# Half of a sequence's cached latents gathered a second time, already turned, for the scores of the sample attention

## The chip, the cores and the metric

The kernel runs on one core of one Trainium2 chip. A core has five engines that run side by side and hand work to one another through semaphores: TensorE (PE) multiplies matrices, VectorE (DVE) and ScalarE (ACT) work on rows of elements, GpSimd (POOL) here does little but issue gathers, and SyncE (SP) issues plain transfers. On-chip data lies in SBUF (128 partitions), matmul results in PSUM. The metric is the device time of one execution in microseconds (us).

## The reference

One inference step of a two-layer decoder, all in float32, for a prompt of 512 tokens and for 8 sample sequences of one token each. Layer 0 is a convolution branch and a gated linear attention, layer 1 a multi-head latent attention, and each is followed by PEER, a retrieval of single-neuron experts. The change is in layer 1, in the attention of the samples over 4096 cached positions. These lie in 32 pages of 128 rows; a page table says which physical page holds which logical one. Cut to what matters:

```python
ckv_past = cache_ckv[j][page_table].reshape(bs, -1, R_KV)     # (8, 4096, 256)
kpe_past = cache_kpe[j][page_table].reshape(bs, -1, D_ROPE)   # (8, 4096, 32)
sp = (einsum('bqhr,bkr->bhqk', q_lat, ckv_past)               # scores: needs r on the partitions
      + einsum('bqhd,bkd->bhqk', q_pe, kpe_past)) * MLA_SCALE
p = softmax(concatenate([sp, s_self]))
o = einsum('bhqk,bkr->bqhr', p[..., :n_past], ckv_past) + ... # weighted sum: needs k on the partitions
```

A matmul sums over the partitions. The scores sum over r, so they want the latents turned (r on the partitions), while the weighted sum wants the rows as they lie in the cache (k on the partitions).

## The kernel before

The stages run one after the other, each a function with its own buffers and semaphores, and a barrier of all engines between them: the layer-0 mixer, PEER, `latent_projections` (buffers `c_`), `latent_sample` (buffers `d_`), PEER again.

**Gathers.** `gather_past(b)` brings a whole sequence b (4.7 MB) into one of three buffers of `smp_past`, with four indirect DMAs issued by POOL, each for eight pages: 128 rows of 9216 bytes (eight keys with their latents and rope keys). The row numbers are worked out near the start of `latent_projections`: the page table comes by DMA, DVE casts it (L1935), PE spreads it over the partitions (L2102), DVE makes row numbers of it (L1937); DVE's `turn_in(0)` (L1864) and PE's first projection come behind that in their queues. At the end of that stage, when the prompt's attention no longer needs `smp_past`, POOL gathers sequences 0 to 2.

**The sample stage.** `latent_sample` walks over b = 0..7. PE's program of one step, in order (each engine's queue is strictly in order):

- `turn_rope(b)` (L2461) turns the rope keys; it waits for all four gathers of sequence b
- `turn_pages(b, g)` for g = 0..7 (L2469): eight 128x128 transposes each, into one of two PSUM turn banks; ACT (L2294, g = 0, 2, 4, 7) or DVE (L2359, g = 1, 3, 5, 6) copies the result into `ckvT`
- between them, what is left of the softmax of sequence b-1: `fold_heads(b-2)`, `turn_max(b-1)` (L2492), `spread_max(b-1)` (L2498)
- `scores(b, 0)` behind g = 5 (L2481 on the latents, L2485 on the rope keys); it waits until ACT has taken the exponentials of b-1 (L2304), which free the score bank
- `turn_weights(b-1)` (L2506), g = 6 and 7, `total_sums(b-1)`, `weighted(b-1)` (L2528, L2529), and last `scores(b, 1)`

DVE takes the largest score (`partial_max`, L2364) after `scores(b, 1)`; before it stands `normed(b-1)`, which scales the result of `weighted(b-1)`. POOL waits until `weighted(b-3)` is done (semaphore `o_ps`) and then issues the four gathers of sequence b into the buffer that this frees. SP loads the output weights into such a buffer when `weighted(5)` is done. After the loop comes the rest of sequence 7 and the output projection (L2588, L2594).

Of the kernel before, what the change touches and what calls it, by code (L numbers as in the profile page):

```python
# [15 lines left out]
I32 = mybir.dt.int32  # L16
# [1611 lines left out]
def latent_projections(nc, w, out, ident, x_sb, smp):  # L1628

    with ExitStack() as ctx:  # L1630
        def sb(name, shape, dt=F32):
# [25 lines left out]
        table_f = sb("table_f", [PAST_PIECE, NB])  # L1657
        spread = sb("spread", [PAST_PIECE, 128])
# [7 lines left out]
        mask = sb("mask", [128, SEQ])  # L1666
        eps = sb("eps", [128, 1])
# [30 lines left out]
            "s_ps", "max_ready", "e_ready", "sum_inv", "p_ready", "pT_ps", "pT_ready", "pv_ps", "o_used", "y_ps", "y_used"))  # L1698
        stores = [sem("stores_even"), sem("stores_odd")]
# [15 lines left out]
        def _(sp):  # L1715
# [3 lines left out]
            for dst, name in ((table, "page_cols"), (spread, "spread"), (part, "sixteenth")):  # L1719
                sp.dma_start(dst[:], w[name]).then_inc(table_in, 16)  # L1720
# [128 lines left out]
        def _(dve):  # L1849
# [84 lines left out]
            dve.wait_ge(table_in, 48)  # L1934
            nc.vector.tensor_copy(table_f[:], table[:]).then_inc(table_ready, 1)  # L1935
# [48 lines left out]
        def _(pe):  # L1984
# [117 lines left out]
            nc.tensor.matmul(ps[0][:, 0:NB], spread[:], table_f[:], start=True, stop=True).then_inc(ids_ps, 1)  # L2102
# [53 lines left out]
def latent_sample(nc, w, ident, x_sb, smp):  # L2156
# [6 lines left out]
    TURNS = G + 2  # L2163
    CKV_BUFS = 6
    with ExitStack() as ctx:
# [26 lines left out]
        ckvT = sb("ckvT", [128, CKV_BUFS, 2, KEYS])  # L2192
# [15 lines left out]
        y_row = sb("y_row", [B, D_MODEL])  # L2208
# [10 lines left out]
        def buf(g):  # L2219
            return ckvT[:, g % CKV_BUFS]  # L2220

# [8 lines left out]
        oT_ps, oT_ready, y_ps, y_rows, y_used = sem("oT_ps"), sem("oT_ready"), sem("y_ps"), sem("y_rows"), sem("y_used")  # L2230
        block = ctx.enter_context(nc.Block())
        KPE, PT = 0, 7
        GROUP_TURN = (1, 2, 3, 4, 5, 6, 8, 9)
# [31 lines left out]
        @block.gpsimd  # L2265
        def _(pool):
            nc.gpsimd.memset(one[:], 1.0).then_inc(consts, 1)
            nc.gpsimd.memset(self_s[:], NEG_MASK).then_inc(consts, 1)
            nc.gpsimd.memset(self_e[:], 0.0).then_inc(consts, 1)
            for b in range(BUFS, B):  # L2270
                pool.wait_ge(o_ps, b - BUFS + 1)
                gather_past(nc, w, smp, b)

        @block.scalar
        def _(act):
# [39 lines left out]
            for b in range(B):  # L2315
                page_out(b, 0)
                if b == 0:
                    latent_queries_out()
                page_out(b, 2)
                if b:  # L2320
                    exps(b - 1)
                page_out(b, 4)
                if b:
                    weights_out(b - 1)
                page_out(b, 7)
# [9 lines left out]
        def _(dve):  # L2335
# [59 lines left out]
            for b in range(B):  # L2395
                rope_out(b)
                if b >= 2:
                    folded(b - 2)
                page_out(b, 1)
                if b:  # L2400
                    largest(b - 1)
                page_out(b, 3)
                page_out(b, 5)
                page_out(b, 6)
                if b == 0:
                    self_out()
                if b:
                    normed(b - 1)
                partial_max(b)
# [10 lines left out]
        def _(pe):  # L2420
# [25 lines left out]
            def turn_free(i, b, half):  # L2446

                before = i - 4 if b == 0 and i == PT + 2 else i - 2
# [23 lines left out]
            def scores(b, half):  # L2472

                for g in range(4 * half, 4 * half + 4):
                    pe.wait_ge(*turned(GROUP_TURN[g], b))
# [3 lines left out]
                for c in range(2):  # L2479
                    for j in range(4):  # L2480
                        nc.tensor.matmul(s_bank[group(j), KEYS * half:KEYS * half + KEYS], qlT[:, c, b, :], buf(4 * half + j)[:, c, :], start=(c == 0), stop=False)  # L2481
# [61 lines left out]
            for b in range(B):  # L2543
# [21 lines left out]
                turn_pages(b, 4)  # L2565
                turn_pages(b, 5)
# [3 lines left out]
                turn_pages(b, 6)  # L2570
                turn_pages(b, 7)
# [3 lines left out]
                scores(b, 1)  # L2575
# [22 lines left out]
PAST_BUFS, PAST_PIECE, PAST_PIECES = 3, 8, NP // 8  # L2598
ROW = PAST_PIECE * (R_KV + D_ROPE)


def sample_buffers(nc, ctx):

    def sb(name, shape, dt=F32):
# [4 lines left out]
            "row_ids": sb("row_ids", [128, DEC_BATCH * PAST_PIECES], I32), "four": sb("four", [128, 4]),  # L2609
# [4 lines left out]
def constants():  # L2614
# [3 lines left out]
    for l in range(LEVELS):  # L2618
# [25 lines left out]
            "low_half": np.stack([p % 32 < 16, p % 32 >= 16], axis=1).astype(np.float32),  # L2644
            "sixteenth": (p % TOPK).astype(np.float32)[:, None]}


def laid_out(a):
# [12 lines left out]
    def low_rows(g):  # L2661
# [19 lines left out]
        "cache_rows": lambda: np.concatenate([a["cache_ckv"][0].reshape(-1, 8 * R_KV), a["cache_kpe"][0].reshape(-1, 8 * D_ROPE)], axis=1),  # L2681
        "page_cols": lambda: np.ascontiguousarray(a["page_table"].reshape(-1, 8).T),
# [17 lines left out]
_USED = ['ab_norm_cols', 'ab_w_in', 'ab_w_out', 'c_kv_norm', 'c_norm_cols', 'c_w_in', 'c_w_out', 'c_w_uk', 'c_w_uv', 'cache_rows', 'causal', 'chan_cols', 'conv_w_cols', 'cos2', 'ffn_norm', 'final_norm', 'fold', 'fold_h', 'four', 'gate_b_cols', 'gla_head_g', 'gate_rows', 'ident', 'iota16', 'keysT', 'level_masks', 'low_half', 'own_col32', 'own_row', 'own_row32', 'page_cols', 'peer_uv0', 'peer_uv1', 'q_norm_cols', 'sin2', 'sixteenth', 'spread', 'spread8', 'state_conv', 'state_conv_cols', 'state_gla', 'turn_q', 'w_q_heads', 'w_qx', 'w_ukT', 'x_prompt', 'x_sample']  # L2700
# [21 lines left out]
```

## Time and profile before

| | |
|---|---|
| median of 3 runs | 3503.63 us (3503.6 to 3508.55) |
| profiled execution, its span from first to last instruction | 3501.1 us |
| the sample stage within it | about 1928.3 to 2150.0 us |
| POOL's gathers in the whole program | 1040 of PEER, 32 of the past |

The span is given from the first to the last instruction; the runs' time is taken by the device around it, so the fastest and the median run lie 2.5 us above it. In the views below a time of start counts from the start of the span. "[x <-Y]" behind an instruction says that its engine was idle for x us before it and that Y ended the wait; "issue" means that nothing the profile shows was waited for, "remote" that the semaphore's last update could be put down to no instruction.

### The profile page before, as it was taken

The numbers are of one execution on the slowest core, as the hardware profiler recorded it, in microseconds if no ns is written. First come the engines' busy times: TensorE is split into PE (matmuls) and PEld (weight loads), VectorE is DVE, ScalarE is ACT, GpSimd is POOL, SyncE is SP. The second block draws the span as 40 slices with busy tenths as digits, with TensorE's granted clock in tenths as the row PEclk, the third lists the DMA queues.
The fourth block names the chain that finished last, engine by engine and source line by source line (L and its number), as shares of the span: only waits on it lengthen the run. The fifth ranks groups of instructions, "written<-read, shape, count | busy, mean of one in ns | idle before, by whom it ended". The sixth has DMA issues, their size and how long they took to land. (4 is left out here: it accounts for less than half of the span.)

```text
span 3501.1 us, 34014 instructions
## 1 busy us (share of the span) xinstructions
PE 2983.7 (85%) x10561; PEld 1480.5 (42%) x10561; DVE 2185.4 (62%) x5266; ACT 1438.0 (41%) x4182; POOL 1301.9 (37%) x1112
## 2 busy tenths in 40 slices
PE   8987888888889888887999886888888888888886
PEld 7653333433334433333554764434333434433332
DVE  4874667666667766664362334666766676766765
ACT  3122445444444544443351222444444444544444
POOL 0211444444544444452001010445444454444442
PEclk9988999999999999999999897999999999999999
DMA  4015999999999999998203345999999999999998
GB/s 163 29 52 228 421 421 414 421 421 415 420 398 421 418 421 421 421 419 350 81 1 162 134 165 220 421 421 414 421 421 421 415 408 421 409 421 421 421 419 355
DMA packets 178372, 1194.53 MB, mean 341 GB/s; under 512 B 22320, under 2 KB 28240, under 8 KB 38150
## 3 DMA queue, kind: packets, MB, share of 16 engines
q0 software_dynamic: 154368, 1128.34, 77.8%
q1 hardware_dynamic: 22525, 63.11, 4.8%
q8 instruction: 84, 1.38, 0.2%
q10 hardware_dynamic: 1296, 0.90, 0.1%
q14 instruction: 99, 0.80, 0.1%
HBM read 1188.29 MB, written 4.46 MB: 341 GB/s over the span
## 5 line engine op out<-in xcount | busy, mean ns | idle before, releaser
L1581 PE MATMUL p_acc<-p_rows,p_diag 128*128 128x512 f32 (+1 forms) x4160 | 1973.0, 616 | 412.8 <-ACT p_diag L1184 411.0
L1414 DVE CUSTOM_DVE_ANT_0 p_rows<-p_rows,p_x_n 128x1024 f32<-128x1024 f32 x1024 | 1243.7, 1223 | 790.5 <-DMA p_rows<-in_peer_uv,p_ids 788.4
L1096 POOL DMA_INDIRECT p_rows<-in_peer_uv,p_ids x1024 | 1217.0, 1188 | 1384.6 <-PE p_acc L1581 1281.6
L1581 PEld LDWEIGHTS p_acc<-p_rows,p_diag 128*128 128x128 f32 (+1 forms) x4160 | 752.9, 192 | 1508.5 <-ACT p_diag L1184 790.8
L1178 ACT ACTIVATE p_acts<-p_dots 128x1 f32<-128x1 f32 x1040 | 208.3, 200 | 871.8 <-DVE p_dots L1414 870.4
L1184 ACT ACTIVATE p_diag<-ident,p_gated 128x128 f32<-128x128 f32 x1024 | 410.9, 401 | 33.6
L1180 ACT ACTIVATE p_gated<-p_acts,p_gates 128x1 f32<-128x1 f32 x1024 | 301.6, 295 | 33.2
L1531 PE MATMUL p_q_bank<-p_w_q,p_xT 128*128 128x256 f32 x1024 | 234.9, 383 | 2.2 <-ACT p_xT L1127 2.2
L1531 PEld LDWEIGHTS p_q_bank<-p_w_q,p_xT 128*128 128x128 f32 x1024 | 196.1, 192 | 55.5 <-issue 28.5
L1150 ACT COPY p_q_rows<-p_q_bank 128x256 f32<-128x256 f32 x68 | 25.2, 370 | 347.7 <-PE p_q_bank L1531 347.7
L1623 POOL DMA_INDIRECT smp_past<-in_cache_rows,smp_row_ids x32 | 30.0, 937 | 361.1 <-PE c_ps L2096 227.4
L1178 ACT ACT_TABLE_LOAD x73 | 93.7, 1283 | 8.7 <-DVE p_dots L1414 7.5
L2469 PE MATMUL d_turn<-ident,smp_past 128*128 128x128 f32 x512 | 78.0, 311 | 15.6 <-DVE d_kpeT L2353 14.4
L541 DVE SCALAR_TENSOR_TENSOR a_conv<-a_u,a_conv_wc,a_conv 128x512 f32<-128x512 f32 x120 | 86.6, 792 | 0.0
L688 PE MATMUL a_ps<-a_xT,a_w_in 128*128 128x260 f32 x384 | 85.7, 384 | 0.1
L1414 DVE DVE_READ_ACCUMULATOR2_ANT p_dots<- 128x1 f32 x1040 | 85.1, 82 | 0.0
L1170 ACT ACT_TABLE_LOAD x64 | 82.1, 1283 | 1.1
L688 PEld LDWEIGHTS a_ps<-a_xT,a_w_in 128*128 128x128 f32 x384 | 72.5, 190 | 11.9 <-issue 0.4
L2469 PEld LDWEIGHTS d_turn<-ident,smp_past 128*128 128x128 f32 x512 | 68.8, 162 | 19.9 <-DVE d_kpeT L2353 16.3
L2359 DVE COPY d_ckvT<-d_turn 128x512 f32<-128x512 f32 x64 | 42.1, 687 | 56.2 <-PE d_turn L2469 56.1
L2294 ACT COPY d_ckvT<-d_turn 128x512 f32<-128x512 f32 x64 | 34.7, 587 | 103.0 <-PE d_turn L2469 103.0
L1088 POOL MEMSET p_eps<- 128x1 f32 x2 | 0.2, 98 | 171.2 <-POOLq L62 171.2
(402 smaller groups left out, 2483.0 us busy)
## 6 DMA issues: line engine op xcount, KB each, us to landing
p_w_q<-in_w_q_heads SPq DMA_DIRECT2D x16, 1024.0 KB, 12.2
p_rows<-in_peer_uv,p_ids POOLq DMA_INDIRECT x1024
a_w_in<-in_ab_w_in SPq DMA_DIRECT2D x6, 1024.0 KB
a_w_in<-in_ab_w_out SPq DMA_DIRECT2D x1, 4096.0 KB
c_arena<-in_c_w_out SPq DMA_DIRECT2D x1, 4096.0 KB, 12.7
smp_past<-in_c_w_out SPq DMA_DIRECT2D x1, 4096.0 KB
a_w_in<-in_ab_w_in SPq DMA_DIRECT2D x4, 1008.0 KB, 21.3
smp_past<-in_w_qx SPq DMA_DIRECT2D x1, 3072.0 KB, 18.6
```

What stands on the lines that cost most here:

```text
L541: ins = nc.vector.scalar_tensor_tensor(out=conv[:, c, 0:SEQ], in0=u[:, c, i:i + SEQ], scalar=conv_wc[:, c, i:i + 1], in1=conv[:, c, 0:SEQ] ...
L688: last = nc.tensor.matmul(ps[bank][:, 512 * b:512 * b + half], w_in[:, k, at:at + 128], xT[:, k, half_of(b)], start=(k == 0), stop=(k == K ...
L1096: nc.gpsimd.indirect_dma_start(out=rows[:, slot % RING, :], out_offset=None, in_=w[f"peer_uv{layer}"], in_offset=bass.IndirectOffsetOnAxis ...
L1170: nc.scalar.activation(ex[:], rel[:], ACT.Exp, accum_out=ex_sum[:]).then_inc(ex_ready, 1)
L1178: nc.scalar.activation(acts[:, i % 4, j:j + 1], dots[:, i % 4, j:j + 1], ACT.Gelu).then_inc(gelud, 1)
L1180: nc.scalar.mul(gated[:, i % 4, j:j + 1], acts[:, i % 4, j:j + 1], gate[:, j:j + 1]).then_inc(gated_ready, 1)
L1184: nc.scalar.mul(diag[:, i % 4, j, 0:n], unit[:], gated[:, i % 4, j:j + 1]).then_inc(diag_ready, 1)
L1414: nc.vector.tensor_tensor_reduce(rows[:, k % RING, 0:D_MODEL], rows[:, k % RING, 0:D_MODEL], x, 1.0, 0.0, ALU.mult, ALU.add, dots[:, slot ...
L1531: last = nc.tensor.matmul(q_bank[:, 0:D_KEY], xT[:, k, :], w_q[:, h, k, :], start=(k == 0), stop=(k == KC - 1))
L1581: last = nc.tensor.matmul(acc[done % 2][0:n, at], diag[:, slot // GROUP % 4, j, 0:n], rows[:, (slot + j) % RING, D_MODEL + 512 * b:D_MODEL ...
L2359: nc.vector.tensor_copy(buf(g)[:, half, :], bank(0, half)).then_inc(turn_dve, 1)
L2469: last = nc.tensor.transpose(turn[i % 2][:, KEYS * c + 128 * a:KEYS * c + 128 * a + 128], latent(b, NQ * g + a, c), ident[:])
```

## The change

The host lays out one more table, `cache_turned`: every page turned, so that row `128 * page + r` holds latent component r of the page's 128 keys (1 KB: both halves of the 256 components, keys ordered by their place in a group of eight). Of every sequence, logical pages 16 to 31 are gathered a second time from this table, 128 rows of 1 KB for each page, into three buffers `turned_c` of eight pages. `scores(b, 1)` reads them in place through an access pattern of runs of 16 elements; `scores(b, 0)` is as before.

- Gone: `turn_pages(b, 4)` to `(b, 7)`, 32 transposes and their four copies on ACT and four on DVE, in each of the eight steps. The numbers of the turns change with them.
- Added: 16 indirect DMAs of 128 KB a sequence on POOL, 128 in all. The first 24 (pieces 0 to 2) stand at the start of the sample stage. Pieces 2b+3 and 2b+4 wait for both scores of step b. **The four gathers of sequence b+2 now stand behind these 16 in POOL's queue.**
- Moved: `scores(b, 1)` stands before `weighted(b-1)`, and `partial_max(b)` before `normed(b-1)`.
- In `latent_projections`: two more small loads on SP (`lane` and a broadcast of the page numbers) ahead of `norm_col`, a wait for all five, and on DVE a cast and a multiply-add for the 128x128 row numbers. Three small tiles move into memory that is free at that time.

```diff
-            for dst, name in ((table, "page_cols"), (spread, "spread"), (part, "sixteenth")):
-                sp.dma_start(dst[:], w[name]).then_inc(table_in, 16)
+            for dst, name in ((table, "page_cols"), (spread, "spread"), (part, "sixteenth"), (lane, "lane")):
+                sp.dma_start(dst[:, :], w[name]).then_inc(table_in, 16)
+            sp.dma_start(smp["turned_ids"][:], w["turned_pages"].to_broadcast([128, 128])).then_inc(table_in, 16)
...
-            dve.wait_ge(table_in, 48)
-            nc.vector.tensor_copy(table_f[:], table[:]).then_inc(table_ready, 1)
+            dve.wait_ge(table_in, 80)
+            nc.vector.tensor_copy(table_f, table[:]).then_inc(table_ready, 1)
+            nc.vector.tensor_copy(pages_f, smp["turned_ids"][:]).then_inc(pages_ready, 1)
+            dve.wait_ge(pages_ready, 1)
+            nc.vector.tensor_scalar(smp["turned_ids"][:], pages_f, 128.0, lane[:], ALU.mult, ALU.add)
...
+        def turned_slots(b, j, c):
+            piece = 2 * b + j // 2
+            by_slot = turned_c[:, piece % TURNED_BUFS].rearrange("p g (c s q) -> p c s g q", c=2, s=KEYS_8)
+            return by_slot[:, c, NQ * (j % 2):NQ * (j % 2) + NQ]
...
-            for b in range(BUFS, B):
-                pool.wait_ge(o_ps, b - BUFS + 1)
-                gather_past(nc, w, smp, b)
+            def gather_turned(piece):
+                if piece >= TURNED_BUFS:
+                    pool.wait_ge(s_ps, 2 * ((piece - TURNED_BUFS) // 2 + 1))
+                for k in range(KEYS_8):
+                    at = KEYS_8 * piece + k
+                    nc.gpsimd.indirect_dma_start(out=turned_c[:, piece % TURNED_BUFS, k, :], out_offset=None, in_=w["cache_turned"],
+                                                 in_offset=bass.IndirectOffsetOnAxis(ap=smp["turned_ids"][:, at:at + 1], axis=0)
+                                                 ).then_inc(turned_in[piece % TURNED_BUFS], 16)
+            for piece in range(TURNED_BUFS):
+                gather_turned(piece)
+            for b in range(B):
+                for piece in (2 * b + TURNED_BUFS, 2 * b + TURNED_BUFS + 1):
+                    if piece < 2 * B:
+                        gather_turned(piece)
+                if BUFS <= b + 2 < B:
+                    pool.wait_ge(o_ps, b)
+                    gather_past(nc, w, smp, b + 2)
...
             def scores(b, half):
-                for g in range(4 * half, 4 * half + 4):
-                    pe.wait_ge(*turned(GROUP_TURN[g], b))
+                if half == 0:
+                    for g in range(4):
+                        pe.wait_ge(*turned(GROUP_TURN[g], b))
+                else:
+                    for piece in (2 * b, 2 * b + 1):
+                        pe.wait_ge(turned_in[piece % TURNED_BUFS], 16 * KEYS_8 * (piece // TURNED_BUFS + 1))
...
-                turn_pages(b, 4)
-                turn_pages(b, 5)
                 scores(b, 0)
                 if b:
                     turn_weights(b - 1)
-                turn_pages(b, 6)
-                turn_pages(b, 7)
+                scores(b, 1)
                 if b:
                     total_sums(b - 1)
                     weighted(b - 1)
-                scores(b, 1)
```

## Rows read from the trace of the kernel before

**Rows 1.** Page: the span and the engines' busy time.

```profile
span 3501.1 us, 34014 instructions
PE 2983.7 (85%) x10561; PEld 1480.5 (42%) x10561; DVE 2185.4 (62%) x5266; ACT 1438.0 (41%) x4182; POOL 1301.9 (37%) x1112
```

**Rows 2.** Windows: us; busy PE, PEld, DVE, ACT, POOL; PE's clock, DMA share, GB/s.

```profile
1973.00:1998.00 25.00, 21.90 (x261) 16.48 (x257) 9.29 (x19) 6.99 (x16) 3.75 (x4) 0.93 0.49 190
...
2098.60:2118.00 19.40, 19.40 (x255) 14.69 (x248) 9.07 (x18) 6.99 (x16) 0.00 (x0) 1.00 0.56 217
```

**Rows 3.** Timeline of POOL: start us, us, engine, instruction, idle time before it.

```profile
1884.65 0.94 POOL L1623 DMA_INDIRECT smp_past<-in_cache_rows,smp_row_ids  x1 [0.30 <-issue]
1928.35 0.09 POOL L2267 MEMSET d_one<- 1x1 f32 x1 [42.76 <-POOLq L62]
...
1998.04 0.94 POOL L1623 DMA_INDIRECT smp_past<-in_cache_rows,smp_row_ids  x1 [19.71 <-PE d_o L2529]
...
2001.77 0.94 POOL L1623 DMA_INDIRECT smp_past<-in_cache_rows,smp_row_ids  x1 [0.31 <-issue]
```

**Rows 4.** Timeline of DVE and PE beside these gathers.

```profile
1884.90 1.22 DVE L1981 TENSOR_TENSOR x_sb<-x_sb,c_ps 128x1024 f32<-128x1024 f32 x1 [14.02 <-PE c_ps L2152]
...
1997.87 0.48 DVE L2389 TENSOR_SCALAR d_o_n<-d_o,d_inv 128x256 f32<-128x256 f32 x1 [3.71 <-PE d_o L2529]
...
1998.92 1.44 PE L2485 MATMUL d_s<-d_kpeT,d_qpT 128*32 128x128 f32 x32
...
2003.85 1.23 DVE L2364 TENSOR_REDUCE d_m<-d_s 128x1 f32<-128x1024 f32 x1 [5.50 <-remote]
```

**Rows 5.** Waits in the sample stage: us in total, times, longest.

```profile
DVE d_m L2364 <- remote: 27.5, 5, 5.5
```

**Rows 6.** The 20 gathers of 1973 to 2078 us, from issue to landing.

```profile
DMA to landing us min/median/max: 8.1/9.7/11.4
```

**Rows 7.** Timeline of step 7, the last, with no gather beside it.

```profile
2101.10 1.09 PE L2461 MATMUL d_turn<-ident,smp_past 128*128 128x128 f32 x8
...
2106.37 0.38 PE L2498 MATMUL d_m<-d_one,d_nmx 1*128 1x1 f32 x2
...
2106.68 1.97 PE L2469 MATMUL d_turn<-ident,smp_past 128*128 128x128 f32 x16
...
2106.97 1.12 ACT L2304 ACTIVATE d_sc<-d_s,d_nbias 128x1024 f32<-128x1024 f32 x1
...
2108.57 1.92 PE L2481 MATMUL d_s<-d_ckvT,d_qlT 128*32 128x512 f32 x16
...
2111.30 1.09 PE L2506 MATMUL d_turn<-ident,d_sc 128*128 128x128 f32 x8
...
2114.09 0.28 PE L2517 MATMUL d_m<-d_sums,d_fold 128*128 128x2 f32 x2
...
2118.47 0.48 DVE L2389 TENSOR_SCALAR d_o_n<-d_o,d_inv 128x256 f32<-128x256 f32 x1 [3.70 <-PE d_o L2529]
...
2119.52 1.44 PE L2485 MATMUL d_s<-d_kpeT,d_qpT 128*32 128x128 f32 x32
...
2120.89 0.62 PE L2540 MATMUL d_m<-d_fold_h,d_o_n 128*128 128x16 f32 x4
...
2122.74 0.27 PE L2492 MATMUL d_m<-ident,d_m 128*1 128x128 f32 x1 [1.23 <-DVE d_olT L2393]
```

**Rows 8.** Timeline of the start of `latent_projections`.

```profile
1644.30 0.35 SPq L1720 DMA_DIRECT2D c_part<-in_sixteenth  x1
...
1649.72 0.17 DVE L1935 CAST c_table_f<-c_table 8x32 f32<-8x32 int32 x1 [2.75 <-DMA c_part<-in_sixteenth]
...
1650.61 0.25 DVE L1937 TENSOR_SCALAR smp_row_ids<-c_ps,c_part 128x32 int32<-128x32 f32 x1 [0.72 <-PE c_ps L2102]
```

**Rows 9.** Transfers: KB each, us to landing.

```profile
c_kv_gain<-in_c_kv_norm SPq DMA_DIRECT2D x1, 128.0 KB, 8.0
```

**Rows 10.** Page, the costliest groups: busy us, mean ns, idle before.

```profile
L1096 POOL DMA_INDIRECT p_rows<-in_peer_uv,p_ids x1024 | 1217.0, 1188 | 1384.6 <-PE p_acc L1581 1281.6
```

More of the change, by code:

```diff
@@ L1656, in latent_projections @@
         table = sb("table", [PAST_PIECE, NB], I32)
-        table_f = sb("table_f", [PAST_PIECE, NB])
-        spread = sb("spread", [PAST_PIECE, 128])
+        table_f = past[0:PAST_PIECE, kT_at + 128:kT_at + 128 + NB]
+        spread = past[0:PAST_PIECE, kT_at + 256:kT_at + 384]
         part = sb("part", [128, 1])
@@ L1666, in latent_projections @@
         mask = sb("mask", [128, SEQ])
+        lane = sb("lane", [128, 1])
+        pages_f = past[:, kT_at:kT_at + 128]
         eps = sb("eps", [128, 1])
@@ L2101, in _ @@
             pe.wait_ge(table_ready, 1)
-            nc.tensor.matmul(ps[0][:, 0:NB], spread[:], table_f[:], start=True, stop=True).then_inc(ids_ps, 1)
+            nc.tensor.matmul(ps[0][:, 0:NB], spread, table_f, start=True, stop=True).then_inc(ids_ps, 1)
             pe.wait_ge(ids_ready, 1)
@@ L2162, in latent_sample @@
     KEYS = NQ * 128
-    TURNS = G + 2
-    CKV_BUFS = 6
+    TURNS = G // 2 + 2
+    HALF = G // 2
     with ExitStack() as ctx:
@@ L2191, in latent_sample @@
         self_s = sb("self_s", [128, B, B])
-        ckvT = sb("ckvT", [128, CKV_BUFS, 2, KEYS])
+        ckvT = sb("ckvT", [128, HALF, 2, KEYS])
+        turned_c = sb("turned_c", [128, TURNED_BUFS, KEYS_8, R_KV])
         kpeT = sb("kpeT", [128, G, 128])
@@ L2230, in latent_sample @@
         oT_ps, oT_ready, y_ps, y_rows, y_used = sem("oT_ps"), sem("oT_ready"), sem("y_ps"), sem("y_rows"), sem("y_used")
+        turned_in = [sem(f"turned_in{i}") for i in range(TURNED_BUFS)]
         block = ctx.enter_context(nc.Block())
-        KPE, PT = 0, 7
-        GROUP_TURN = (1, 2, 3, 4, 5, 6, 8, 9)
+        KPE, PT = 0, 5
+        GROUP_TURN = (1, 2, 3, 4)
         def turn_count(i, b, half):
@@ L2446, in turn_free @@
             def turn_free(i, b, half):
-                before = i - 4 if b == 0 and i == PT + 2 else i - 2
+                before = i - 2
                 if before >= 0:
@@ L2480, in scores @@
                     for j in range(4):
-                        nc.tensor.matmul(s_bank[group(j), KEYS * half:KEYS * half + KEYS], qlT[:, c, b, :], buf(4 * half + j)[:, c, :], start=(c == 0), stop=False)
+                        dst = s_bank[group(j), KEYS * half:KEYS * half + KEYS]
+                        if half == 0:
+                            nc.tensor.matmul(dst, qlT[:, c, b, :], buf(j)[:, c, :], start=(c == 0), stop=False)
+                        else:
+                            nc.tensor.matmul(dst.rearrange("h (s g q) -> h s g q", s=NQ, g=KEYS_8), qlT[:, c, b, :], turned_slots(b, j, c), start=(c == 0), stop=False)
                 for a in range(NQ):
@@ L2598 @@
 PAST_BUFS, PAST_PIECE, PAST_PIECES = 3, 8, NP // 8
+TURNED_BUFS = 3
 ROW = PAST_PIECE * (R_KV + D_ROPE)
```

18 lines of the change are left out of this document (9 added, 9 removed).

## The prediction

> **What bounds the kernel now.** I read the page first [rows 1]: PE is busy for 85% of the span, but that is an average over stages that have different limits, and the change touches one stage of some 220 us. So the windows of that stage came next [rows 2]. A step with gathers beside it takes 25.0 us, PE busy for 21.9; the last step, with none, takes 19.4 us and PE is never idle. PE is the bound, and something that comes with the gathers costs 5 to 6 us a step. POOL works 3.75 us of a step. It is nowhere near a limit.
>
> The timelines say what the 5 us are [rows 3, 4]. PE ends the last matmul of scores(2, 1) at 2000.4 us, DVE's maximum, which waits for nothing else, starts at 2003.85, after 5.5 us of idle time. POOL ended its fourth gather at 2002.71, 1.1 us earlier. All five such steps look alike (27.5 us of DVE idle time in all [rows 5]); what holds PE's word back I cannot tell from the trace. It is no fixed price of a POOL that is issuing: during the first twelve gathers DVE started its addition at 1884.90, right after PE, while POOL was inside a gather [rows 3, 4].
>
> The third thing to read is POOL's pitch [rows 3]: gathers back to back start (2001.77 - 1998.04) / 3 = 1.243 us apart, 0.94 of it work.
>
> **What the change removes.** 32 of 64 page transposes a step. At full clock 16 of them take 1.97 us [rows 7], so PE saves 3.9 us. Of that only part shortens the step. Pages 4 and 5 hid the exponentials of the step before: spread_max ends at 2106.75, ACT's exponentials run 2106.97 to 2108.1, and scores(b, 0) began at 2108.57 in any case. Without the pages it waits for ACT and begins at 2108.2. From there 2.7 us of scores, 1.3 of turned weights and 3.0 of scores(b, 1): from the start of turn_rope(b) to the end of scores(b, 1) I get 14.1 us. With 4.1 for total_sums and weighted(b-1), until its last matmul has ended (2114.09 to 2118.4) a step of PE is 18.2 us, against some 19.8 before (2101.10 to 2120.96). The 16 copies a step on ACT and DVE lie beside it and give nothing.
>
> **What it adds.** 16 gathers a step. A 1 KB row is in no row of POOL's; PEER's gathers of 8 KB rows and these of 9 KB take the same 0.94 us when nothing stretches them (PEER's mean of 1.19 is of all of its gathers, whatever runs beside them) [rows 3, 10], so I take 0.94 and a pitch of 1.243. Lower bound: the 0.3 us between two gathers alone. Upper bound: PEER's mean, pitch 1.49. **20 gathers are 24.9 us a step on POOL: POOL, not PE, sets the step.** The transfers themselves are small (128 KB every 1.24 us).
>
> **Where it hurts: the queue.** Before, the four gathers of sequence b+2 were issued as soon as weighted(b-1) was done, a whole step ahead. Now they stand behind 16 others, and turn_rope(b+2) waits for all four. POOL starts in the sample stage at 1928.7 (three memsets after 1928.35). Ahead of the gathers of sequence 7 stand 24 + 6 x 16 + 4 x 4 = 136 gathers: 169.0 us, so 2097.7. The fourth is issued 3.7 us later and lands 11.4 us after that (the longest, since POOL's queue is full around it) [rows 6]: 2112.8. Another 14.1 us of PE: scores(7, 1) end at 2126.9. Before they ended at 2119.52 + 1.44 = 2120.96 [rows 7]. **+5.9 us.**
>
> This supposes that POOL never waits. From the first gather of sequence b+2 to the end of scores(b+2, 1) is 3.7 + 11.4 + 14.1 = 29.2 us; POOL's own work in the same time is 24 gathers, 29.8. There are 0.6 us to spare. But PE now stands idle for some 6 us of each step, and behind idle time the granted clock falls to 1.2 GHz: in a step in which PE was idle for 3.1 us it was 0.93 over 25.0 us [rows 2], half speed for 3.5 us, which loses some 1.7 us of work; twice as long would lose 3.4. I take 2.5. Then the path misses POOL by 1.9 us; such a delay is carried through every second step (3 and 5), and the low clock counts once more in step 7: 2 x 1.9 + 2.5 = **+6.3 us** (0 to 9.0).
>
> **The moved lines.** weighted(6) now stands between scores(7, 1) and the last softmax. Before, turn_max(7) came 1.8 us after the scores [rows 7]; now 4.1 of sums and weighted, 0.5 of DVE's scaling, 0.6 of fold_heads and a copy (0.3, an estimate) [rows 7] come first, with the hand-overs 5.9. **+4.1 us.** What follows is unchanged. The output weights (4 MB) are loaded when weighted(5) is done, now about 2110, while the gathers of sequence 7 are still landing; 3.5 us shared would cost up to 3.5, I take **+2**.
>
> **The first stage.** DVE started on the page table when the third small load had landed, 5.4 us after its issue, which took 0.35 [rows 8]. Two more loads issued before the wait: some +0.8. The new DVE work (a 128x128 cast and a multiply-add) hides in the 0.72 us in which DVE waits for PE's spread of the table. The broadcast of the page numbers may be slower: kv_gain, the nearest one, took 8.0 us to land [rows 9], which would make it +3.4. I take **+1**. PE's first projection waits behind this.
>
> **How the strided read counts.** scores(b, 1) reads runs of 16 elements. If that halved PE's rate on its latents, 1.9 us more [rows 7], it would count like the clock, 3 times: +5.7. No row shows it; I take 0 and keep 5.7 for the range.
>
> **Sum.** 5.9 + 6.3 + 4.1 + 2 + 1 = 19.3 us on a span of 3501.1, and with 2.5 us between span and median 3503.6 + 19.3 = **3523 us**. The case's own range is 5.9 + 4.1 + 0.8 = 10.8 to 5.9 + 9.0 + 4.1 + 3.5 + 3.4 + 5.7 = 31.6: 3514 to 3535.
>
> **The rivals.** *POOL's issue is cheap (faster).* If a gather of short rows costs POOL little more than the 0.3 us gap, PE sets the step: scores(0, 1) at about 1954, seven steps of 18.2 end at 2081, 39.5 us before today; with 4.1 and 1 given back 3469. It decides where the pitch falls below about 1.05: 139 gathers times 0.19 are the 26 us between my sum and -7. Against it: every unstretched gather in the trace is 0.94, for two row sizes. 0.08. The Trainium skill leans this way: DMA: Bandwidth & Descriptors, in its anatomy of one DMA, calls descriptor generation "small, variable" and says that many descriptors can be emitted before the cost shows. The trace doesn't agree for POOL's time, 0.94 us for 128 rows.
>
> *Only POOL's count binds (no change to tell).* If the four gathers land 6 us sooner than 11.4, the last piece sets the end: 148 x 1.243 = 184.0, landed by about 2115.4, scores 3.0: 2118.4, which is -2.6; with 4.1 and 1: 3506. Against it: 8.1 is the shortest landing of any, and the fourth is always the latest. 0.13.
>
> *PE's word is held back during the new gathers too (much slower).* If PE's signals to ACT and DVE were stuck until 1.1 us after POOL's last gather in all of this stage, a step would be 20.7 us of 16 gathers, 6 of the four, then 13 of PE: 40 us instead of 25. Five such steps, with 34 and 24 for the two shorter ones and the first from about 1983, end at 2241: 3628. For it: five of five in this stage. Against it: the addition at 1884.90. 0.11.
>
> *DVE stretches the gathers (slower).* At PEER's mean pitch of 1.49, 139 x 0.25 = 35 us more: 3558. Against it: DVE's scaling from PSUM (L2389) ran beside the first of the four gathers, which kept 0.94 [rows 3, 4]; the other four steps repeat this. 0.06. The Trainium skill's SBUF — State Buffer, under who interferes with whom, says that DVE's copies can take the port that GpSimd writes its descriptors through; no copy of the stage lies beside a gather in this trace.
>
> **How the numbers follow.** My forecast has 0.62. Within 0.2% (7 us, about what a measurement of this kernel can tell) I put 0.11: the second rival, less its upper edge. Faster 0.09, the first rival and a little of the second. Slower 0.80. The range leaves out most of the first, all of the third and half of the fourth rival: 3497 to 3548.
>
> **What would show it.** POOL: gathers 1.24 us apart with hardly a gap from 1928.7 to about 2115, of 0.94 us each. PE: its longest wait in steps 3 to 7 is before turn_rope(b), for the landing of the gathers of the past, and not before scores(b, 1) for the turned pieces. The clock is at half speed behind it. DVE's maximum starts right behind the scores again. Scores(b, 1) take the same 3 us as scores(b, 0). In `latent_projections` the cast starts about 1 us later. I am wrong if the pitch is under 1.05 (faster), if PE waits for the turned pieces alone (about no change), or if the idle time "remote" grows with POOL's bursts (much slower).

## The result, and the profile after

The changed kernel takes 3613.67 us (median of 4 runs), the kernel before beside it 3505.35 us. The ratio is 1.0309, 95% interval 1.0294 to 1.0324: 3.1% slower. I had forecast slower, by 19 us; it is 108. The time lies near my third rival (3628 us, chance 0.11).

The page's span, and of the waits those of 1928 to 2261 us (us in total, times, longest):

```profile
span 3612.7 us, 33562 instructions
...
ACT d_ckvT L2326 <- remote: 128.0, 5, 26.5
DVE d_o_n L2419 <- remote: 117.4, 6, 21.5
```

These answer to [rows 1, 5]. By the page PE is busy for 2995.5 us, 12 us more than before; POOL, at 1423.1, has 121 us more of work, which is not on the path. Before, words of PE that came late cost DVE 27.5 us. Now they cost ACT 128 us and DVE 117, side by side. The windows of a step with all 20 gathers (us; busy PE, PEld, DVE, ACT, POOL; PE's clock, DMA share, GB/s) answer to [rows 2]:

```profile
2049.70:2087.55 37.85, 20.89 (x222) 13.85 (x222) 6.52 (x14) 5.05 (x12) 18.89 (x20) 0.77 0.52 181
```

37.9 us instead of 25.0 for less work of PE, DVE and ACT. The timeline of one step, with the engines sorted together (start us, us, instruction, idle time before it):

```profile
2011.51 1.22 DVE L2394 TENSOR_REDUCE d_m<-d_s 128x1 f32<-128x1024 f32 x1 [21.39 <-PE d_s L2521]
2011.75 0.94 POOL L2292 DMA_INDIRECT d_turned_c<-in_cache_turned,smp_turned_ids  x1 [9.76 <-PE d_s L2521]
2017.44 0.38 PE L2565 MATMUL d_o<-smp_ckv,d_self_pT 128*32 128x256 f32 x1 [0.79 <-issue]
2024.61 0.37 PE L2497 MATMUL d_turn<-ident,smp_past 128*128 128x128 f32 x1 [1.03 <-issue]
...
2030.50 0.95 POOL L2292 DMA_INDIRECT d_turned_c<-in_cache_turned,smp_turned_ids  x1 [0.30 <-issue]
...
2034.65 0.48 DVE L2419 TENSOR_SCALAR d_o_n<-d_o,d_inv 128x256 f32<-128x256 f32 x1 [21.45 <-remote]
2034.75 1.07 ACT L2326 COPY d_ckvT<-d_turn 128x512 f32<-128x512 f32 x2 [26.50 <-remote]
2034.81 0.94 POOL L1623 DMA_INDIRECT smp_past<-in_cache_rows,smp_row_ids  x1 [3.36 <-remote]
...
2049.70 1.22 DVE L2394 TENSOR_REDUCE d_m<-d_s 128x1 f32<-128x1024 f32 x1 [7.72 <-PE d_s L2521]
```

Read it in this order. DVE's maximum and POOL's first gather start right behind the scores. PE ends weighted(b-1) at 2017.8, the rope keys and the first group of pages by 2025.0, and then waits for DVE's scaling of weighted(b-1). ACT has nothing to do and starts on that first group at 2034.75; DVE's scaling of a result that PE ended at 2017.8 starts at 2034.65; POOL's wait for the same word ends at 2034.81. Three engines go on within 0.2 us of one another, 3.2 us after POOL's last gather of the run, on words that PE owed them: from the end of weighted(b-1) to DVE's scaling it is 16.8 us here and 17.5 us in the step that begins at 2125.25. From the first gather to that moment it is 22.9 us for 16 gathers. It was 5.8 us for the four of [rows 3, 4]. It is 34.2 for the run of 24 with which the stage begins, and 11.7 for the last run of eight:

```profile
1931.88 0.96 POOL L2292 DMA_INDIRECT d_turned_c<-in_cache_turned,smp_turned_ids  x1 [0.43 <-issue]
1966.09 1.29 DVE L2389 COPY d_ckvT<-d_turn 128x512 f32<-128x512 f32 x2 [30.07 <-remote]
...
2202.49 0.95 POOL L2292 DMA_INDIRECT d_turned_c<-in_cache_turned,smp_turned_ids  x1 [11.64 <-PE d_s L2521]
2214.23 0.48 DVE L2419 TENSOR_SCALAR d_o_n<-d_o,d_inv 128x256 f32<-128x256 f32 x1 [10.28 <-remote]
```

That is 1.43 to 1.47 us for each gather of a run, where POOL needs 1.25. PE's own matmuls suffer too: from 2016 us on they start in clumps with gaps of 0.2 to 1.0 us in which PE waits for nothing that the profile shows.

### The profile page after: what moved, and what is told of

It is laid out like the page before. It is cut to its first block and busy times, and to the rows that moved or that the text cites. A ratio compares the mean times of both kernels' runs of the same rounds, so it can differ in the third digit from the quotient of the medians.

```text
span 3612.7 us, 33562 instructions
## 1 busy us (share of the span) xinstructions
PE 2995.5 (83%) x10305; PEld 1470.2 (41%) x10305; DVE 2166.4 (60%) x5236; ACT 1421.6 (39%) x4150; POOL 1423.1 (39%) x1240
## 5 line engine op out<-in xcount | busy, mean ns | idle before, releaser
L2292 POOL DMA_INDIRECT d_turned_c<-in_cache_turned,smp_turned_ids x128 | 121.1, 946 | 119.6 <-PE d_s L2521 82.6
L2326 ACT COPY d_ckvT<-d_turn 128x512 f32<-128x512 f32 x32 | 18.0, 588 | 183.2 <-remote 128.0
L2497 PE MATMUL d_turn<-ident,smp_past 128*128 128x128 f32 x256 | 55.7, 370 | 23.9 <-issue 23.3
L1154 ACT COPY p_qT<-p_q_bank 128x256 f32<-128x256 f32 x64 | 23.8, 372 | 90.0 <-PE p_q_bank L1545 89.8
## 6 DMA issues: line engine op xcount, KB each, us to landing
p_w_q<-in_w_q_heads SPq DMA_DIRECT2D x16, 1024.0 KB, 12.1
```

What stands on the lines that cost most here:

```text
L2292: nc.gpsimd.indirect_dma_start(out=turned_c[:, piece % TURNED_BUFS, k, :], out_offset=None, in_=w["cache_turned"], in_offset=bass.Indirect ...
L2497: last = nc.tensor.transpose(turn[i % 2][:, KEYS * c + 128 * a:KEYS * c + 128 * a + 128], latent(b, NQ * g + a, c), ident[:])
```

## The experiments

They ran in five jobs, each on one chip with the kernel before beside it. The kernel before told two kinds of job apart: 3505.9, 3505.5 and 3502.1 us in three, 3477.2 and 3477.1 us in two. One chip ran a job of either kind, so the kind isn't a property of the chip, as the expectations had it. I call the three *stuck* and the two *free*, for what the traces show. In the last of the three only kernels with spaced gathers have a trace; that it is a stuck one rests on the kernel before, 3502.1 us beside them, and on words of PE up to 1.0 us late in the changed kernel with fills, where the same kernel in the free jobs has 0.1. A ratio is to the kernel before of the same job.

**What the change does where nothing is stuck.** Both kernels, unchanged, ran again, in a stuck and in a free job.

> The kernel before, unchanged, to have its profile beside runs of the changed one on one chip. The runs so far were on two chips: on one the kernel before took 3505.9 us, on the other 3477.2, and on that other one a kernel with four gathers in a row at 1.25 us showed no late words of PE. Chip theory: whether PE's words get stuck during POOL's gathers is a property of the chip. On a chip of the first kind this profile shows five waits of DVE of 5.5 us for a late word and some 3504 us, on one of the second kind none, steps of 19.8 us and some 3477 us.

> The changed kernel, unchanged. On a chip of the first kind 3613 us, steps of 38 us and PE's words 10 to 17 us late. On one of the second kind nothing holds PE's words; what is left is POOL's pace, 20 gathers x 1.25 = 25 us a step, and the gathers of the past behind the turned ones: by the prediction's own sum scores(7, 1) end at about 2127 to 2133 and the kernel takes 3510 to 3520, slower than the kernel before there by 35 to 40 us, since that one loses nothing to late words.

Measured, in a stuck job: 3505.2 and 3612.0 us (ratio 1.0308, 1.029 to 1.0325), as in the first result. The kernel before has five waits of DVE of 5.5 us, and the changed one words of PE up to 17.9 us late.

> The changed kernel, unchanged, once more, for the chip of the second kind, on which it has not run (its mark is a time of some 3477 us of the kernel before beside it). There, if late words of PE are all that my forecast missed, the profile shows no word of PE more than 1 us late, POOL's gathers 1.25 us apart with hardly a gap, PE's longest waits before turn_rope for the gathers of the past, and scores(7, 1) ending at about 2127 to 2133; the kernel takes 3505 to 3520. On a chip of the first kind 3612 us again.

> The kernel before, for its profile on the same chip as the run above. On a chip of the second kind: no wait of 5.5 us of DVE for a late word, steps of 19.8 us throughout, 3477 us. On one of the first kind 3505 us.

Measured, in a free job: 3476.7 us for the kernel before, 3521.6 us for the changed one (1.0124, 1.0107 to 1.0141). Steps of the kernel before, at DVE's maximum, in the free job (the timeline):

```profile
1979.22 1.23 DVE L2364 TENSOR_REDUCE d_m<-d_s 128x1 f32<-128x1024 f32 x1 [2.08 <-PE d_s L2485]
1999.01 1.23 DVE L2364 TENSOR_REDUCE d_m<-d_s 128x1 f32<-128x1024 f32 x1 [2.10 <-PE d_s L2485]
```

19.8 us with gathers beside them, as the one without had in [rows 7]: the 5.5 us of [rows 4] are gone, and the kernel is 28 us faster by that alone. Of the changed kernel in the free job, PE's longest wait, POOL's only waits of the stage, the landing of all 32 gathers of the past, and the last maximum:

```profile
PE d_turn L2489 <- DMA smp_past<-in_cache_rows,smp_row_ids: 35.2, 13, 7.0
...
2030.42 0.95 POOL L2292 DMA_INDIRECT d_turned_c<-in_cache_turned,smp_turned_ids  x1 [1.71 <-PE d_s L2521]
2081.40 0.94 POOL L2292 DMA_INDIRECT d_turned_c<-in_cache_turned,smp_turned_ids  x1 [1.30 <-PE d_s L2521]
...
DMA to landing us min/median/max: 6.1/11.1/23.9
...
2135.57 1.23 DVE L2394 TENSOR_REDUCE d_m<-d_s 128x1 f32<-128x1024 f32 x1 [7.72 <-PE d_s L2521]
```

No word of PE is more than 0.2 us late. Here the steps of my working are to be seen: POOL is the bound and waits twice, 1.7 and 1.3 us, behind the scores of steps 3 and 5; PE waits for the gathers of the past; the last scores end at 2135.5, where I had 2126.9 + 6.3 = 2133.2. Of the 20 gathers of this stage the landing is 6.1/10.0/14.2 us; the 23.9 belongs to the twelve before it. The kernel ends at 3521.6; the forecast was 3523.

**Is it the pitch of the gathers?** POOL gets a fill behind each of the four gathers in the kernel before; `pacer` only waits for its own last fill before the next.

```diff
                 pool.wait_ge(o_ps, b - BUFS + 1)
-                gather_past(nc, w, smp, b)
+                gather_past(nc, w, smp, b, pace)     # behind each gather: nc.gpsimd.memset(idle[:], 0.0), 128 x 512
```

> The kernel before, with a fill of 128x512 zeros on POOL behind each of the four gathers of sequences 3 to 7, so that they start some 1.8 us apart instead of 1.24. If a gather takes some 1.4 us of the way that PE's words need, and the words are stuck only because gathers come faster than that, they now pass between the gathers: a step falls from 25.0 to some 20 us, the kernel to about 3480. If the words are stuck for as long as POOL's run lasts, whatever its pitch, the run is 2 us longer and so is the step: about 3513.

Measured, in a stuck job: 3480.7 us, ratio 0.9931 (0.9915 to 0.9948). The gathers start 1.64 us apart and DVE's maxima 20.5:

```profile
1977.08 0.94 POOL L1637 DMA_INDIRECT smp_past<-in_cache_rows,smp_row_ids  x1 [47.42 <-PE d_o L2547]
1978.72 0.94 POOL L1637 DMA_INDIRECT smp_past<-in_cache_rows,smp_row_ids  x1 [0.16 <-issue]
...
2000.75 1.23 DVE L2382 TENSOR_REDUCE d_m<-d_s 128x1 f32<-128x1024 f32 x1 [2.83 <-PE d_s L2503]
2021.27 1.22 DVE L2382 TENSOR_REDUCE d_m<-d_s 128x1 f32<-128x1024 f32 x1 [2.83 <-PE d_s L2503]
```

The word is 1.0 us late instead of 3.6. More work for POOL, in a longer run of gathers, gives 25 us: the run's length doesn't hold the words. That it is the distance between the gathers, and not something else that a fill between them does, is how I read it; no run made the distance without a fill.

> The kernel before with a fill of 128x256 instead of 128x512 behind each of the four gathers: they start some 1.38 us apart, between 1.24 (words stuck, step 25.0 us) and 1.64 (words at most 1.0 us late, step 20.5 us). If a gather takes 1.42 us of the way that the words need, gathers at 1.38 still fill it and the words stay stuck nearly as long: 3495 to 3505. If only the idle time between two gathers counts, the words are late by about half as much: near 3490. If any fill in between frees the way, 3480.

Measured: 3477.0 us, 0.9999 (0.999 to 1.0009). It fell into a free job, where nothing is stuck at 1.25 us either. It says nothing of the bound between 1.25 and 1.64.

The same in the changed kernel, three fills of 128x64 behind each gather of the stage:

> The changed kernel with three small fills of 128x64 zeros on POOL behind every gather of the sample stage, 144 gathers in all, so that they start some 1.6 to 1.8 us apart instead of 1.25. POOL gets slower by 50 to 70 us over the stage. If PE's words and matmuls are stuck only while gathers follow each other faster than about one in 1.42 us, they now get through, POOL alone sets the step (20 x 1.7 = 34 us against 38) and the kernel is faster than the changed one all the same: 3560 to 3595. If the words are stuck in any run of gathers, the runs are now 27 us long instead of 20 and the kernel slower: 3650 or more.

> The changed kernel with three small fills behind each gather, so that they start 1.69 us apart. On the chip of the second kind it took 3579 us and POOL's pace set the step, 33.8 us. If on a chip of the first kind the fills free PE's words, it takes the same 3579 us there, 33 us less than the changed kernel although POOL is slower. If a run of gathers holds the words whatever its pitch, 3650 or more there.

> The changed kernel with gathers 1.69 us apart, once more, now hoping for a chip of the first kind (3505 us of the kernel before beside it), on which it has not run. If the wider pitch frees PE's words there, some 3579 us, as on two chips of the second kind, and faster than the changed kernel's 3612 us with a slower POOL; no word of PE more than 1 us late. If the words are held in any run of gathers, whatever its pitch, 3650 us or more.

Measured: 3579.0 and 3578.3 us in the two free jobs, 3578.7 us in a stuck one (1.0216, 1.0199 to 1.0233). The stuck one:

```profile
2034.04 0.95 POOL L2310 DMA_INDIRECT d_turned_c<-in_cache_turned,smp_turned_ids  x1
2035.72 0.95 POOL L2310 DMA_INDIRECT d_turned_c<-in_cache_turned,smp_turned_ids  x1
...
PE d_turn L2508 <- DMA smp_past<-in_cache_rows,smp_row_ids: 73.9, 20, 9.8
```

The kind of job no longer matters. With a POOL that needs 1.68 us a gather the changed kernel is 33 us faster in a stuck job than with one that needs 1.25, and what PE waits for is the gathers of the past, 74 us in all. In a free job the same fills cost 57 us. Both signs come from the same edit: this is the experiment that separates stuck words from POOL's pace. The 33 us compare two stuck jobs, since the changed kernel without fills had no run beside this one.

**Is it the queue?** The gathers of the past ahead of the turned ones:

```diff
             for b in range(B):
+                if BUFS <= b + 2 < B:
+                    pool.wait_ge(o_ps, b)
+                    gather_past(nc, w, smp, b + 2)
                 for piece in (2 * b + TURNED_BUFS, 2 * b + TURNED_BUFS + 1):
                     if piece < 2 * B:
                         gather_turned(piece)
-                if BUFS <= b + 2 < B:
-                    pool.wait_ge(o_ps, b)
-                    gather_past(nc, w, smp, b + 2)
```

> The changed kernel with one line of POOL's program moved: in each step the four gathers of sequence b+2 are issued before the 16 of turned pages. Queue theory (the prediction's: the gathers of the past are late because they stand behind the turned ones): their delay and the low clock behind it go, 5.9 + 6.3 us back, 3601. Held-word theory (the words that PE sends to ACT and DVE are stuck until POOL's whole run of gathers is over): the run is now 20 gathers without a gap and begins only when weighted(b-1) has ended, some 4 us later; the words come about 1.42 x 20 = 28.4 us after its first gather instead of 22.8, so a step is some 8 to 10 us longer and the kernel slower than the changed one: 3645 to 3665.

> The changed kernel with the gathers of sequence b+2 ahead of the turned ones. On a chip of the first kind 3617 us. On one of the second kind POOL still needs 25 us a step, but the four gathers of the past land early and the step is POOL's 25 us plus its wait for weighted(b-1): by the queue theory no longer than in the changed kernel, 3500 to 3515.

Measured, both in stuck jobs: 3617.6 us (1.0319, 1.0302 to 1.0337) and 3618.4 us (1.0323). Neither theory's number. The queue theory falls in a stuck job: what it moves isn't what binds. In a free job this order had no run, so there the queue is read from the trace and wasn't varied. But a run of 20 gathers doesn't hold all words to its end either. The run that starts at 2054.60 us:

```profile
2060.28 0.58 ACT L2326 COPY d_ckvT<-d_turn 128x512 f32<-128x512 f32 x1 [3.38 <-PE d_turn L2497]
2061.72 0.58 ACT L2326 COPY d_ckvT<-d_turn 128x512 f32<-128x512 f32 x1 [0.85 <-remote]
2063.17 0.69 DVE L2389 COPY d_ckvT<-d_turn 128x512 f32<-128x512 f32 x1 [4.35 <-remote]
2066.02 0.16 ACT L2330 COPY d_nbias<-d_m 128x1 f32<-128x1 f32 x1 [3.71 <-remote]
...
2073.82 0.27 PE L2521 MATMUL d_s<-d_kpeT,d_qpT 128*32 128x128 f32 x1 [1.06 <-issue]
2075.22 0.27 PE L2521 MATMUL d_s<-d_kpeT,d_qpT 128*32 128x128 f32 x1 [1.13 <-issue]
```

PE had executed all that these copies wait for by 2059.7. Its words come out one at a time, 1.4 us apart at first and 0.7 to 2.1 us after that (DVE's second copy starts at 2065.31), and later matmuls start singly, 1.4 and 2.1 us apart. So PE isn't shut off; what it sends, and then what it executes, comes some 0.7 us or a multiple of it apart while gathers follow one another closely. My picture "held until the run is over" may be this, seen where PE had much to send; no run shows that the two are one.

**What is PE's saving worth?** Only the first three pieces gathered:

```diff
             for b in range(B):
-                for piece in (2 * b + TURNED_BUFS, 2 * b + TURNED_BUFS + 1):
-                    if piece < 2 * B:
-                        gather_turned(piece)
...
-                        pe.wait_ge(turned_in[piece % TURNED_BUFS], 16 * KEYS_8 * (piece // TURNED_BUFS + 1))
+                        pe.wait_ge(turned_in[piece % TURNED_BUFS], 16 * KEYS_8)
```

> The changed kernel without the turned gathers behind the first three pieces: scores(b, 1) of the later sequences read old pieces, so the scores of their second half are not computed from their own latents. PE, ACT and DVE execute what they do in the changed kernel. It prices PE's saving alone. Queue theory and held-word theory both expect the steps to fall from 38 us; if the four gathers of the past still hold PE's words for 3 to 4 us a step, the step is about 23.5 us and the time about 3530; if PE alone sets it, 18.2 us a step and about 3493. If the changed kernel's loss were in PE's own program (the strided read, the moved lines), the time would stay above 3580.

Measured, in a stuck job: 3499.9 us (0.9985, 0.9976 to 0.9995). The windows of step 1, of the last step and of one with the four gathers:

```profile
1979.89:1993.69 13.80, 11.90 (x150) 8.39 (x148) 5.56 (x11) 4.96 (x12) 0.00 (x0) 1.00 0.01 2
2099.83:2117.71 17.88, 16.30 (x222) 11.37 (x222) 6.58 (x14) 4.96 (x12) 0.00 (x0) 1.00 0.62 237
2035.94:2056.83 20.89, 17.75 (x222) 11.62 (x222) 6.58 (x14) 4.87 (x12) 3.75 (x4) 0.92 0.58 227
```

13.8 us without weighted(b-1), 17.9 with it: I had 14.1 and 18.2. PE's program is as short as worked out; four gathers in a row still cost 3.0 us of each step, and the first run of 24 some 25 us.

**Another engine for the gathers.** SP loads a page's row number into a register and issues a plain transfer; POOL keeps the four gathers of a step.

```diff
+                    for k in range(KEYS_8):
+                        at = KEYS_8 * piece + k
+                        row = nc.values_load(smp["turned_ids"][0:1, at:at + 1], engines=[SP], ...)
+                        sp.dma_start(turned_c[:, piece % TURNED_BUFS, k, :], w["cache_turned"][bass.ds(row, 128), :]).then_inc(turned_in[piece % TURNED_BUFS], 16)
```

> The changed kernel with the turned pages fetched by SP instead of POOL: for each page SP loads its row number into a register and issues one plain transfer of 128 rows of 1 KB. POOL is left with the four gathers of a step, as before. Held-word theory: only those four hold PE's words, the first scores no longer wait for a run of 24 gathers, and a step is 18 to 24 us: 3465 to 3506, if SP manages 16 pages in a step. If loading a number and issuing take SP more than 1.2 us a page, SP sets the step: at 1.65 us a page 26.4 us a step, about 3520. If the turned transfers themselves (not POOL's issuing) hold PE, the time stays near 3600.

Measured, in a stuck job: 3506.7 us (1.0008, 0.9998 to 1.0018), 107 us less than the changed kernel. The same bytes reach the same place, so it is the issuing on POOL and not the moving of these bytes that holds PE. POOL's four gathers of a step, 1.25 us apart, still do: words of PE up to 2.4 us late. What is left is SP's pace (timeline, transfers of a stretch in one row) and PE's wait for a turned piece:

```profile
1929.61 26.77 SPq L2279 DMA_DIRECT2D d_turned_c<-in_cache_turned  x24
...
1994.76 3.34 PE L2514 MATMUL d_s<-d_turned_c,d_qlT 128*32 128x512 f32 x16 [3.97 <-issue]
```

26.77 us for 24 pages, 1.1 us each. With the eight numbers of a piece loaded by one instruction ahead of the wait:

> The kernel in which SP fetches the turned pages, with the eight row numbers of a piece loaded by one instruction ahead of the wait, instead of one by one between the transfers. In the run with single loads SP spent 1.1 us on a page, and PE waited 3 to 4 us a step for the turned pieces. If that pitch was what PE waited for, a page now takes 0.5 us and the step falls from 24.5 to about 21 us, as in the kernel without turned transfers: some 3480. If the pieces come late because the 4.7 MB of the past go ahead of them in the DMA engines, the step stays at 24 us: about 3505.

> The same, and POOL's four gathers of a step spaced by three small fills. If both causes add, the words of PE are no longer stuck and the step is near PE's own 18 us: 3460 to 3470. If the past's transfers hold up the turned ones, 3480 to 3490, as fast as the kernel before with spaced gathers.

Measured, in a free job: 3471.6 us (0.9984, 0.9974 to 0.9994) and 3471.2 us (0.9981). A page now takes 15.0 / 24 = 0.62 us, the steps are 17.9 us, and spacing adds nothing where nothing is stuck. The last step is 25.3 us; in `sp_batch`:

```profile
1932.74 14.98 SPq L2280 DMA_DIRECT2D d_turned_c<-in_cache_turned  x24
...
2065.82 0.39 SPq L2291 DMA_DIRECT2D smp_past<-in_c_w_out  x1
...
2082.71 3.24 PE L2515 MATMUL d_s<-d_turned_c,d_qlT 128*32 128x512 f32 x16 [6.08 <-issue]
```

PE stands for 6.1 us before scores(7, 1): the last piece is behind 4 MB of output weights. The next edit puts the weights behind it.

```diff
             for b in range(B):
-                if b == B - 2:
-                    sp.wait_ge(o_ps, B - 2)
-                    sp.dma_start(w_out, ...).then_inc(wout_in, 16)
                 sp_gather(p for p in (2 * b + TURNED_BUFS, 2 * b + TURNED_BUFS + 1) if p < 2 * B)
+            sp.wait_ge(o_ps, B - 2)
+            sp.dma_start(w_out, ...).then_inc(wout_in, 16)
```

> The kernel in which SP fetches the turned pages with numbers loaded eight at a time, with the load of the output weights behind the last turned piece instead of before it. Where that kernel took 3471.6 us its last step was 25.3 us instead of 17.9, and PE waited 6.3 us in it for the last turned piece, which stands behind 4 MB of weights in SP's queue. If that is the reason, the last step falls to about 18 us: 3464 to 3466 on a chip of the second kind, and some 20 us more on one of the first kind, where the four gathers of the past hold PE's words for 2 to 3 us a step.

> The fastest version put together: SP fetches the turned pages, the output weights come behind the last of them, and three small fills space POOL's four gathers of a step. Without the fills it took 3486.0 us on a chip of the first kind, with PE's words up to 4.0 us late and five steps of 21.7 to 23.0 us instead of 17.9. If spacing frees the words, 3464 to 3468 on either kind of chip.

> The version put together, once more. On a chip of the second kind it took 3461.5 us. On one of the first kind, where it took 3486.0 us with PE's words up to 4.0 us late before the four gathers of a step were spaced, it should take 3462 to 3468 us, 1.2% less than the kernel before, if spacing frees the words.

Measured: without fills 3486.0 us in a stuck job (0.9945, 0.9929 to 0.9962), the last step 17.9 us, so the weights were the reason, and words of PE at most 2.5 us late by its trace, where the expectation of the next run says 4.0; with them 3461.5 us in a free one (0.9954, 0.9937 to 0.997) and 3461.3 us in a stuck one (0.9883, 0.9867 to 0.99). In the stuck one:

```profile
2023.31 1.23 DVE L2409 TENSOR_REDUCE d_m<-d_s 128x1 f32<-128x1024 f32 x1 [7.72 <-PE d_s L2536]
2041.19 1.23 DVE L2409 TENSOR_REDUCE d_m<-d_s 128x1 f32<-128x1024 f32 x1 [7.72 <-PE d_s L2536]
```

17.9 us a step (one of them 18.1), in either kind of job the fastest version of all: 16 us below the kernel before where no word is stuck, and 41 us where they are, if POOL neither issues the turned gathers nor its own back to back. Of the 41 us the turned pages are the smaller part: spacing POOL's gathers alone gave the kernel before 25 us in a stuck job (`paced_before`).

## Why the prediction was wrong

**The step that failed** is the supposition under "Where it hurts" that only POOL's count and the queue set the time, with PE's words free during the new gathers: late words are a term that the sum has at nothing. I gave the case in which they are late 0.11. It gave 40 us a step and 3628; measured are 38 us and 3613.7, with words of PE up to 17.5 us late in five steps. Of the 40 us, 20.7 for the run of 16 is 22.9; the 6 us for the four gathers of the past don't appear, since PE's next words pass during them (DVE and ACT start on PE's transposes at 2037.20 and 2039.12 while they are issued or just behind); and PE's 13 us are 15, part of them at half clock.

**Why I gave it so little.** For it stood five runs of gathers out of five in this very stage; against it one addition of DVE in another stage [rows 4]. Beside that one PE executes long matmuls, 128x512, and sends DVE a word in some 14 us; here it executes matmuls of 128x128, some 0.12 us each, besides the long ones, and sends several words a step. The stage in which the new gathers were to lie had only witnesses for it. I let one from elsewhere outweigh them because I had no mechanism.

**The queue (+5.9, +6.3).** Not what binds in the result. In the free job it comes near what I worked out: the last scores end at 2135.5 against 2121.0 of [rows 7] in the kernel before, +14.5 where I had 12.2; the profiled times of the stage's start agree within 0.2 us. The parts: the fourth gather of sequence 7 starts at 2105.14, 3.7 us behind the 2101.4 of a POOL that never waits (3.0 of it POOL's two waits); it lands after 14.2 us and not 11.4; and from there to the end of the scores it is 16.2 us and not 14.1, with PE at half clock at first (0.50 from 2116.0 to 2125.0). That the forecast of 3523 us is met there (3521.6) is half luck: the kernel before is 28 us faster in such a job, so the difference is 44 us and not 19. My sum was made on a step of 25.0 us that held 5.5 us of stuck words, and it silently took them out of the new step.

**Gather of 1 KB rows (0.94, pitch 1.243).** 128 of them, 0.946 us median, pitch 1.25. The Trainium skill's DMA: Bandwidth & Descriptors, which calls descriptor generation "small, variable", isn't borne out for POOL's time. *POOL's issue is cheap* and *DVE stretches the gathers* both fall.

**PE's step without the transposes (18.2).** 17.9 us. Right, and unused.

**The strided read (0).** Right. Of the step that ends at 2049.70:

```profile
2042.97 1.92 PE L2515 MATMUL d_s<-d_ckvT,d_qlT 128*32 128x512 f32 x16 [1.58 <-ACT d_sc L2336]
2046.84 1.92 PE L2517 MATMUL d_s<-d_turned_c,d_qlT 128*32 128x512 f32 x16
```

L2517 reads the turned pages in runs of 16 elements, L2515 the contiguous copy.

**The moved lines (+4.1).** In the free job, from DVE's last maximum to the end of the stage 33.1 us (2135.57 to 2168.7) against 28.9 (2121.05 to 2150.0) in the profile that the forecast was made from: +4.2, at nearly the same granted clock (0.74 and 0.71). In the free job the kernel before needs 25.7 for it at 0.80 (2097.99 to 2123.7), which makes +7.4; how much of that is the clock, no run separates.

**The output weights (+2).** Near. PE waits for the weights themselves nowhere, but the term was for the landing that they share: their load is issued at 2110.20, between the issue (2105.14) and the landing (2119.3) of the last gather, and that one takes 14.2 us where the fourth gathers of the four sequences before took 11.0 to 12.1. The DMA engines are full in that stretch (share 1.0). No run moved the weights in this kernel, so that these 2 to 3 us are theirs is likely and not shown.

**The first stage (+1).** +1.7 us at DVE's L1868, +1.3 at the start of the sample stage, once the 1.5 us by which the stage began later are taken off:

```profile
1644.60 0.38 SPq L1721 DMA_DIRECT2D c_arena<-in_c_w_in  x1
...
1652.93 0.17 DVE L1939 CAST smp_past<-c_table 8x32 f32<-8x32 int32 x1 [4.45 <-DMA smp_turned_ids<-in_turned_pages]
```

The cast comes 8.3 us after the stage's first load, 6.6 before; it waits for the broadcast of the page numbers.

**What stays open.** Why closely spaced gathers let PE's words through so slowly, and why in some jobs only, on one chip too. That PE's density matters is argued from where it happens and where not, and no run varied it. One page offers a mechanism: the Trainium skill's NOTIFIC — the notification-queue block, The write path, says of the block that writes an engine's trace records that its internal pipeline always holds back rather than lose a record, and that a stall count above zero would mean that it had throttled an engine. PE has two recorded instructions a matmul here. All executions had their records taken, so no run shows whether words are stuck without them.

## What to carry to other kernels

A stall that a trace shows beside every instance of some operation, in the stage that gets more of this operation, is to be scaled with it, even where its cause is unknown; a counterexample counts only if the engines around it do the same things. Look at the wait called "remote" first: a consumer that starts late on a producer long done, at the same distance from a third engine's work in every step, is the sign. Gathers of 128 rows on POOL started 1.25 us apart here, with rows of 1 KB as with rows of 9 KB, so gather few large ones. A start 0.4 us later for each (1.64 us apart) paid where words were stuck, 25 us in the kernel before; in a free job, with 20 gathers a step, it cost 57 us. Many small gathers whose rows lie together in the source can go to SP (0.62 us a page with the numbers loaded ahead). And time an experiment only against the kernel before in the same job.

## What the runs showed of the hardware

- With gathers 1.25 us apart PE's words to ACT, DVE and POOL came late in the result's trace and in both stuck jobs that ran such gathers, by up to 17.9 us (`after_again`); in the free jobs by 0.3 us at most. With gathers 1.64 to 1.69 us apart and fills between them it was at most 1.0 us in a stuck job, in either kernel.
- Words of DVE and ACT weren't late in the same stretches: inside the run of gathers from 1982.28 to 2001.98 us ACT reads out its sums until 1992.26 and PE, which waits for ACT, starts at 1992.41; without gathers beside them, in the step that ends at 2049.70, it is 2042.83 and 2042.97.
- A step of SP's own: one load of eight registers and eight transfers take 5.0 us, eight single loads with their transfers 8.9.
- The same kernel on the same chip: 3477.2 us in one job, 3502.1 in another. Between the profiles of the kernel before of either kind the spans differ by 25.8 us (3501.1 and 3475.3) and the sample stages by 26.9 (1928.35 to 2150.0, and 1928.93 to 2123.7).
